# On-demand float32 gather for expert pairs, and nine prefetch places instead of six, in a two-layer trunk with an expert-choice MoE

## What is computed

```python
cap = CAPACITY_FACTOR * T // N_EXPERTS
aff = jax.nn.softmax((h @ w_router).astype(jnp.float32), axis=-1)
g, idx = lax.top_k(jnp.swapaxes(aff, 1, 2), cap)
xg = jax.vmap(lambda xb, ib: xb[ib])(h, idx)
a = jnp.einsum('becd,edf->becf', xg, w_gate)
u = jnp.einsum('becd,edf->becf', xg, w_up)
y = jnp.einsum('becf,efd->becd', jax.nn.silu(a) * u, w_down) * g[..., None].astype(h.dtype)
return jax.vmap(lambda yb, ib: jnp.zeros((T, D), yb.dtype).at[ib.reshape(-1)].add(yb.reshape(-1, D)))(y, idx)
```

## Time and profile before

| what | us |
|---|---|
| median of 3 runs | 1944.04 (1941.34 to 1945.4) |
| the profiled execution | 1943.38 |
| its span | 1941.6 |
| TensorE matmul busy | 1756.0 (90%) |
| VectorE, ScalarE, GpSimd busy | 640.1, 548.5, 514.2 |
| moved by DMA | 567.78 MB |

### The profile page before, as it was taken

How to read it: one execution, slowest core, us unless ns; L and a number is a source line. 1 busy time by engine, 2 the same in 40 slices (tenths; PEclk the granted TensorE clock), 3 DMA queues, 4 the chain that set the end, 5 groups by cost and what they waited for, 6 DMA issues and landing times.

```text
span 1941.6 us, 22758 instructions
## 1 busy us (share of the span) xinstructions
PE 1756.0 (90%) x9190; PEld 1121.8 (58%) x9190; DVE 640.1 (33%) x1385; ACT 548.5 (28%) x1054; POOL 514.2 (26%) x654
## 2 busy tenths in 40 slices
PE   6999999999998888888889999999999978888887
PEld 3888997898542222222268889879965322222223
DVE  3196345873300000001144853558641000000011
ACT  4434353342321110110144344433332111111011
POOL 1787244373100000000047754424830000000000
PEclk9999999999999999999999999999999999999999
DMA  9635434556999999999963354354656999999996
GB/s 359 160 109 196 156 124 151 182 219 235 364 388 427 426 427 428 426 427 426 411 203 130 109 200 164 116 183 171 247 206 261 426 427 426 426 426 427 428 426 251
DMA packets 121512, 567.78 MB, mean 292 GB/s; under 512 B 21824, under 2 KB 31296, under 8 KB 96320
## 3 DMA queue, kind: packets, MB, share of 16 engines
q1 hardware_dynamic: 110624, 543.91, 70.8%
q10 hardware_dynamic: 9920, 20.84, 2.9%
q0 software_dynamic: 864, 1.58, 0.2%
HBM read 550.57 MB, written 15.73 MB: 292 GB/s over the span
## 4 chain that ended last, share of the span: by engine, by line
PE 55%; DMA 35%; DVE 7%; ACT 2%; issue 1%; POOL 0%; ACTq 0%; SPq 0%; DVEq 0%
PE banks L806 29%; PE banks L1376 11%; DMA work<-in_w_gate 8%; DMA ring<-in_w_up 6%; DMA work<-in_w_up 6%; DMA ring<-in_w_down 6%; DMA ring<-in_w_gate 4%; DMA work<-in_w_down 3%; PE banks L1124 1%; PE banks L1345 1%; PE banks L812 1%; PE banks L818 1%; PE banks L838 1%; ACT work L1481 1%; PE banks L1140 1%; DMA work<-in_x_sample 1%
## 5 line engine op out<-in xcount | busy, mean ns | idle before, releaser
L747 POOL TENSOR_TENSOR ring_fp32r<-ring,ring_fp32r 128x256 fp32r<-128x256 f32 x592 | 462.4, 815 | 825.8 <-ACT ring_fp32r L1481 825.1
L1376 PE MATMUL banks<-ring,work 128*64 128x512 f32 x1776 | 404.2, 599 | 77.2 <-DMA ring<-in_w_gate 33.0
L806 PE MATMUL banks<-xT_fp32r,ring_fp32r 128*128 128x384 f32 x1280 | 346.4, 343 | 1.9 <-POOL ring_fp32r L747 1.9
L1481 ACT ACTIVATE work<-banks 32x512 f32<-32x512 f32 (+6 forms) x400 | 202.8, 528 | 438.6 <-PE banks L1376 251.0
L1376 PEld LDWEIGHTS banks<-ring,work 128*64 128x64 f32 x1776 | 122.9, 137 | 336.6 <-issue 200.2
L1376 PE MATMUL banks<-work 128*64 128x512 f32 x972 | 225.5, 600 | 38.6 <-DMA work<-in_w_gate 13.8
L806 PEld LDWEIGHTS banks<-xT_fp32r,ring_fp32r 128*128 128x128 f32 x1280 | 234.9, 190 | 12.8 <-issue 5.3
L806 PE MATMUL banks<-hT_fp32r,ring_fp32r 128*128 128x384 f32 x640 | 215.9, 337 | 0.0
L2406 DVE SCALAR_TENSOR_TENSOR xT<-banks,mod,xT 128x128 f32<-128x128 f32 (+1 forms) x128 | 47.1, 413 | 443.5 <-PE banks L1412 443.1
L1481 ACT ACTIVATE ring_fp32r<-ring 128x1024 fp32r<-128x1024 f32 (+1 forms) x164 | 154.4, 970 | 76.5 <-PE banks L806 66.7
L1376 PEld LDWEIGHTS banks<-work 128*64 128x64 f32 x972 | 67.4, 137 | 178.7 <-issue 112.4
(11 more groups left out here) (298 smaller groups left out, 1702.4 us busy)
## 6 DMA issues: line engine op xcount, KB each, us to landing
ring<-in_w_up SPq DMA_DIRECT2D x38, 2048.0 KB, 30.6
ring<-in_w_gate SPq DMA_DIRECT2D x37, 2048.0 KB, 30.5
ring<-in_w_down SPq DMA_DIRECT2D x36, 2048.0 KB, 30.0
ring<-in_w_in SPq DMA_DIRECT2D x28, 2048.0 KB, 8.4
ring<-in_w_ada SPq DMA_DIRECT2D x20, 2048.0 KB, 8.5
work<-in_w_down SPq DMA_DIRECT2D x20, 2048.0 KB, 30.5
work<-in_w_gate SPq DMA_DIRECT2D x18, 2048.0 KB, 30.5
work<-in_w_up SPq DMA_DIRECT2D x16, 2048.0 KB, 30.6
```

The lines of the kernel that those rows point to most:

```text
L747: ins = pool.tensor_tensor(rounded(w_), w_, rounded(hi_), ALU.subtract)
L806: mm = pe.matmul(dst, a_, b_, start=(first and i == 0), stop=(last and i == 2))
L1376: mm = pe.matmul(dst[64 * hf:64 * hf + 64, :], x(k), w[kk][:, 512 * hf:512 * hf + 512], start=(k == 0), stop=(k == KC - 1), tile_position= ...
L1481: return act.activation(dst, src, ACT.Copy, scale=scale)
```

## The change

The tokens of each pair of experts are gathered in plain float32 when they are needed. H2MH, GpSimd's low parts, the xf detour with its transposes and the one big gather go. `gather(pair, half)` has twelve matmuls of 64 columns (four strides, three token tiles), with the strided H2M stationary; pair 0 is done ahead of expert 0, pair 1 after `expert_u(0)` and in e = 1, and the rest one half after each `expert_u`. XG shrinks to two pairs, SEL to two pairs, SELG to four experts. The gate matrices are turned four experts at a time (`TURN_GATES`), three transposes each. The room holds slots 4, 6, 7 and 8. Slot 8 is used once (half 0), then its place takes YS and YP; the other eight are reused in turn.

```diff
-SLOTS = RING + 3
-FIRST_SLOTS = ((4, 3, 2, 5, 0, 1), (4, 1, 2, 3, 0, 5))
+SLOTS = RING + 5
+FIRST_SLOTS = ((8, 4, 6, 7, 3, 2, 5, 0, 1), (8, 4, 6, 1, 7, 2, 0, 3, 5))
...
+    return FIRST_SLOTS[l][i] if i < 9 else FIRST_SLOTS[l][1 + (i - 9) % 8]
...
+TURN_GATES = (3, 7, 11, 14)
```

The SP queue in layer 0 (`if l < L - 1`), then in layer 1, then for both:

```diff
                     sp.wait_ge(sem["bp_evac"], 8 * (l + 1))
                     load_rows(l, 0)
+                    load_rows(l, 1)
                     sp.wait_ge(sem["wo_out"], 8 * l + 4)
                     load(("mix", l, 28), dr["w_ada"][l + 1], 512)
+                    load_rows(l, 2)
+                    load_rows(l, 3)
                     sp.wait_ge(sem["wo_out"], 8 * (l + 1))
                     load(("mix", l, 29), dr["w_ada"][l + 1], 1024)
-                    load_rows(l, 1)
+                    load_rows(l, 4)
                     sp.wait_ge(sem["ada_part"], EARLY * (l + 1) + 1)
                     load(("mix", l, 30), dr["w_ada"][l + 1], 1536)
                     sp.wait_ge(sem["ada_part"], EARLY * (l + 1) + 2)
-                    load_rows(l, 2)
+                    load_rows(l, 5)
                     sp.wait_ge(sem["h2t_out"], 6 * (l + 1))
-                    load_rows(l, 3)
-                    load_parameters(l + 1)
+                    load_rows(l, 6)
                     sp.wait_ge(sem["ada_part"], EARLY * (l + 1) + 3)
-                    load_rows(l, 4)
+                    load_rows(l, 7)
                     sp.wait_ge(sem["ada_part"], EARLY * (l + 2))
-                    load_rows(l, 5)
+                    load_rows(l, 8)
                 else:
                     sp.wait_ge(sem["bp_evac"], 8 * (l + 1))
-                    load_rows(l, 0)
-                    load_rows(l, 1)
+                    for i in range(5):
+                        load_rows(l, i)
                     sp.wait_ge(sem["wo_out"], 8 * l + 4)
-                    load_rows(l, 2)
+                    load_rows(l, 5)
                     sp.wait_ge(sem["wo_out"], 8 * (l + 1))
-                    load_rows(l, 3)
-                    load_rows(l, 4)
+                    load_rows(l, 6)
+                    load_rows(l, 7)
                     sp.wait_ge(sem["h2t_out"], 6 * (l + 1))
-                    load_rows(l, 5)
-
-                for i in range(6, NW):
-                    if i == 10:
-                        sp.wait_ge(sem["sgt_out"], 3 * (l + 1))
+                    load_rows(l, 8)
+
+                for i in range(9, NW):
                     load_rows(l, i)
+                    if i == 24 and l < L - 1:
+                        load_parameters(l + 1)
```

TensorE:

```diff
+                def gather(pair, half):
+
+                    bank = 2 + half if pair == 0 else 7
+                    pe.wait_ge(sem["sel_ready"], 8 * l + pair + 1)
                     for c in range(4):
+                        for o, ts in ((0, (1, 2)), (64, (0,))):
+                            for t in ts:
+                                mm = pe.matmul(PS[:, bank, 128 * c + o:128 * c + o + 64], strided(H2M[:, t, 512 * half:512 * half + 512], c),
+                                               SEL[pair % 2][:, t, :, :].rearrange("p a b -> p (a b)"), start=(t == ts[0]), stop=(t == ts[-1]))
                     mm.then_inc(sem["xg_out"], 1)
...
+                def gather_next(pair, half):
+
+                    pe.wait_ge(sem["xg_evac"], 16 * l + 2 * pair + half)
+                    if combined[0]:
+                        pe.wait_ge(sem["x_ready"], 32 * l + combined[0])
+                    gather(pair, half)
...
+                gather_more()
                 for e in range(1, NE):
                     units = COMBINED.get(e, ())
                     expert_a(e)
                     if units:
                         combine_early(units[0])
-                    if e == 1:
-                        pe.wait_ge(sem["sgt_evac"], 3 * (l + 1))
                     expert_down(e - 1)
                     if units:
                         combine_early(units[1])
+                    if e == 1:
+                        gather_more()
                     expert_u(e)
+                    gather_more()
+                    if e in TURN_GATES:
+                        turn_gates(TURN_GATES.index(e))
```

More of the change, by code:

```diff
@@ L409, in trunk_program @@
         GT = [v.rearrange("p (a b) -> p a b", a=3) for v in GT]
-        RSTD = W2[:, 0:T]
+        RSTD = work[:, 0:T]
         QF = QKT.rearrange("p a b -> p (a b)")
@@ L424, in MPL @@
             return KRAW if i < 3 else NAQK[:, 1:3, 256:512]
-        m = region(0, WORK)
-        XG = m([KC, NE, 2, 32])
-        base_sel = m.at[0]
+        m = region(0, base_qk + KC * T)
         H2M = m([TT, D])
-        H2MH = m([TT, D])
-        SEL = m([TT, NE, 32])
-        SELG = m([TT, NE, 32])
+        XG = [m([KC, 2, 2, 32]) for _ in range(2)]
+        base_hidden = m.at[0]
+        HH = m([2, 512])
+        HTT = m([2, 4, 128])
+        SEL = [m([TT, 2, 32]) for _ in range(2)]
+        SELG = m([TT, 4, 32])
+        SG = m([2, T])
         POS = m([TT, NE])
         AFF = m([TT, NE])
+        base_topk = m.at[0]
         AFT = m([T])
@@ L438, in trunk_program @@
         MSK = m([T])
-        end_sel = m.at[0]
-        HH = m([2, 512])
-        HTT = m([2, 4, 128])
+        m = region(base_topk, base_topk + 3 * T)
         TH = m([512])
         SA = m([512])
-        end_hidden = m.at[0]
-        SLOT4 = m([SLOT])
+        m = region(base_qk + KC * T, WORK)
         SLOT5 = m([D])
[L448 to L454, removed]
+        EXTRA = {4: m([SLOT]), 6: m([SLOT]), 7: m([SLOT])}
+        base_y = m.at[0]
+        EXTRA[8] = m([SLOT])
+        m = region(base_y, WORK)
+        YS = m([2, D])
+        YP = m([2, D])
         RRAW = AFT
         def MPE(layer):
-            v = work[:, base_gates:base_gates + 2048] if layer == 0 else work[:, end_hidden - 1024:end_hidden]
+            v = work[:, base_gates:base_gates + 2048] if layer == 0 else work[:, base_hidden:base_hidden + 1024]
             return v.rearrange("p (a b) -> p a b", b=512)
@@ L466, in expert_rows @@
                 return [hT[:, 0:8, :].rearrange("p a b -> p (a b)")[:, D * k:D * k + D] for k in range(3)] + [SLOT5]
-            v = ring[:, slot, :] if slot < RING else (SLOT4 if slot == 4 else SLOT6)
+            v = ring[:, slot, :] if slot < RING else EXTRA[slot]
             return [v[:, D * k:D * k + D] for k in range(4)]
@@ L594, in load_rows @@
                     return
-                dst = ring[:, slot, :] if slot < RING else (SLOT4 if slot == 4 else SLOT6)
+                dst = ring[:, slot, :] if slot < RING else EXTRA[slot]
                 sp.dma_start(dst, w.rearrange("(p k) n -> p (k n)", k=4)).then_inc(landed[slot], 16)
@@ L783, in _ @@
                 low_parts(NQ)
[L784 to L789, removed]
             for n, k in (("k", 2), ("v", 2), ("C", 4), ("m", 2), ("ssm", 1)):
@@ L1337, in strided @@
                     return v.rearrange("p (n k) -> p k n", k=4)[:, c, :]
[L1339 to L1348, removed]
@@ L1352, in _ @@
[L1352 to L1359, removed]
@@ L1369, in project @@
+                combined = [0]
+                gather(0, 0)
+                gather(0, 1)
+                def project(dst, i, x, gathered=None):
                     for half in range(2):
+                        if gathered is not None:
+                            pe.wait_ge(sem["xg_evac"], gathered + half)
                         slot, v = LANDING[("expert", l, i + half)]
@@ L1397, in expert_down @@
                         pe.wait_ge(sem["ht_evac"], g)
+                    turned = sum(at < e + 1 for at in TURN_GATES)
+                    if turned:
+                        pe.wait_ge(sem["sgt_evac"], 4 * l + turned)
                     for c in range(4):
@@ L1421, in _, with gather_more @@
                     ada_select(l + 1, 3)
-                pe.wait_ge(sem["xg_evac"], 18 * l + 2)
                 expert_a(0)
                 expert_u(0)
-                pe.wait_ge(sem["sel_ready"], 3 * (l + 1))
                 if l < L - 1:
                     pe.wait_ge(sem["ada_taken"], EARLY * (l + 2))
[L1429 to L1443, removed]
+                gathered = [2]
+                def gather_more():
+                    if gathered[0] < 16:
+                        gather_next(gathered[0] // 2, gathered[0] % 2)
+                        gathered[0] += 1
+                gather_more()
                 for e in range(1, NE):
@@ L1771, in _ @@
                     act.wait_ge(sem["h2t_out"], 6 * l + g + 1)
-                    copy(rounded(H2MH[:, t, 512 * half:512 * half + 512]), PS[:, g, :])
                     copy(H2M[:, t, 512 * half:512 * half + 512], PS[:, g, :]).then_inc(sem["h2t_evac"], 1)
@@ L1776, in _, with take_gathered @@
                     ada_evacuate(l + 1, 3)
-                for half in range(2):
-                    act.wait_ge(sem["xf_out"], 2 * l + half + 1)
-                    copy(XF[0:64, half, :], PS[0:64, half, :]).then_inc(sem["xf_evac"], 1)
```

(52 more changed lines are left out.)

48 lines of the change are left out of this document (16 added, 32 removed).

## The result

The changed kernel takes 2012.99 us (median of 4 runs, 2010.94 to 2017.38) against 1943.8 us of the kernel before: a ratio of 1.0364, 95% interval 1.035 to 1.0378. I had forecast 1919. The profiled execution is the slowest of the four (span 2015.6, before 1941.6), so its stages sum to some 74 us more where the medians say 69.

What follows compares the result with a forecast made beforehand. The DMA stream of weight halves was taken to bound the expert stages. Nine halves ahead give -10.3 us in layer 0 and -14.2 in layer 1, together -24.5 from 1943.4: 1918.9, said as 1919, range 1912 to 1934.

Steps and rivals of the forecast that it cites:

- The bound: Expert stages: the DMA stream of 96 weight halves sets their end; nine halves ahead shorten its last hole.
- rival C: First gathers run at the lower clock or leave small holes: 6 us a layer, 1931 us; chance 0.10.
- The gather's price: Float32 gather on TensorE: 24 records at 0.119 us, 2.9 us a gather; ends 2.7 and 5.5 us.
- g: Time of one gather of twelve float32 matmuls, 24 records on TensorE: put at 2.9 us.
- the 22 us of cover: Layer 1: TensorE's expert work would end at 1885, the weight stream at 1907, hiding 1.6 us more per gather.
- rival A: TensorE becomes the bound: H2M loads at 0.231 us, gathers of 5.5 us, +6.5 us, 1950 us; chance 0.09.
- Its start of the experts: Under slow H2M loads of 0.231 us, the experts start at 521.7 in layer 0 and 1472.1 in layer 1.
- The parameters: Next layer's parameters, moved into the full stream at half 24: 4.2 us put down, ends 1.7 and 10.1.
- Rival B: Parameters cost the whole SP queue hold, stopping the stream up to 10 us: 1925 us; chance 0.17.
- Half 12 and half 16: Weight stream: their places free at S plus 20.4 and 38.5, DMA ready at 21.9 and 41.6; no hole.
- Rival D: Half 9 or those behind it wait for something else in order; no change, 1943 us; chance 0.05.
- the old hole: Weight stream before the change: half 10 goes out behind the gather, at 544.24 and 1493.08, after the stream's last hole.

Runs made afterwards that it cites:

- the contiguous kernel: The changed kernel with H2M written by ScalarE in the order the gather reads it, so the gather's stationary operand is contiguous: 1919.4 us, ratio 0.9872.
- the run with 128 columns: The changed kernel, stride of four kept, with each gather matmul moving 128 columns of SEL instead of 64: 1960.75 us, ratio 1.009.

## Why the prediction was wrong

**The bound, right.** The stream of weights ruled the kernel before, and more places shorten its last hole. With the gather made cheap, the kernel takes 1919.4 us where the sum of the prediction gives 1919. That it is so close is partly luck. Layer 1 of the contiguous kernel needed 445.1 us from the first gather to the last landing where I had 1907.0 - 1460.3 = 446.7, 1.6 us less. Layer 0 needed 967.0 - 510.2 = 456.8 where I had 961.1 - 508.8 = 452.3, 4.5 us more: its first experts took 16.75 us on the chain, against 13.88 in layer 1, at a granted clock of 0.73 from 518 to 528 us (the slow first expert of rival C), and the parameters cost more than I put down. The runs on that chip were 1 us faster to begin with.

**The gather's price, wrong: the step that failed.** "I take 0.119, since it has the type and the stride of the new one." The row was one of transposes, and a transpose does not pay for a stride as a matmul does. The other row, the old gather at 0.231, I called a far end since its 448 columns were part of its pace; yet it was the row with the same operand and the same kind of instruction, and the truth was 0.234: g = 5.79 us for 2.9. With it the 22 us of cover were gone and TensorE became the bound. Of two rows that disagree, the same operand under the same instruction was the nearer one, and the rule of the Trainium skill's page "SBUF — State Buffer" stood on its side.

The trace of the kernel before could have told. 24 records of 384 columns took 4.17 us in the projections (L806), 0.174 us each, so 448 columns by themselves come to 0.174 x 448 / 384 = 0.203 us, less than 0.231; the run with contiguous fp32r operands then took just that, (9.53 - 0.37) / 45 = 0.204. And its load records say where the rest comes from, contiguous in the projections and strided in the gather:

```profile
L806 PEld LDWEIGHTS banks<-work_fp32r,ring_fp32r x768: 186/188/192, 405.9 to 1430.8; 128*128 128x128 f32 x192
...
L1345 PEld LDWEIGHTS banks<-work_fp32r x96: 308/330/337, 530.3 to 1490.3; 128*128 128x128 f32 x96
```

The 0.007 us that I read as the price of the stride compared transposes with matmuls; against contiguous transposes it is 0.011.

**No term for the clock, wrong.** The fall of the clock behind each gather, 24 us in layer 0 and, by the run with 128 columns, 52 us in all, was in no term and in no rival but as the lower clock at the first gathers and 3 us for a slow first expert (C). So rival A, the mechanism that happened, was mis-sized: 1950 where it came to 2013. Without the clock it would have been 1961 (the run with 128 columns), 11 us over rival A, whose g was 5.5 us for 5.79 (and whose terms add up to 457 us, not 456). Its start of the experts, 521.7, was met (522.8).

**The parameters, mis-sized.** 4.2 us put down; the move ahead of the experts saved 9 us by the medians (1919.4 to 1910.3, on two chips whose kernels before differ by 0.5), 6.5 of it in the time from half 9 to the last landing (439.4 to 432.9 us in layer 0). The SP queue was held 16.8 us (594.6 to 611.35), not 10.1. Rival B had this mechanism, at 6 us more than the forecast.

**The rest.** The experts of the contiguous kernel started at 517.7 in layer 0 for 516.4. Half 12 and half 16 opened no hole. Rival D did not happen. What is left of the old hole lies ahead of half 9: from 518 to 528 us in the contiguous kernel the DMA moved nothing, all nine halves being in.

## What to carry to other kernels

Lay the stationary operand of a matmul out so that at least two of its float32 values share 16 bytes; where a copy out of PSUM makes it anyway, the permutation was free here (the ScalarE copies of 128 x 512 took 601 ns before and 595 ns permuted; stride four to one was worth 94 us). When small matmuls go between large ones, count what they do to the clock behind them, not their own time alone. And put loads of many small rows where the queue has nothing else to issue: that was worth 9 us here.

## What the runs showed of the hardware that I had not expected

- Float32 matmuls of 64 columns with a 128 x 128 stationary operand come 0.11 us a record apart at a stride of one, 0.12 at two and 0.23 at four; fp32r ones of 448 columns come 0.23 apart at a stride of four and 0.20 at one. Transposes come 0.12 apart at a stride of four and 0.11 at one.
- The granted clock fell in gathers of 64 columns under loads of 0.23 us, at each of the fourteen of a layer, but neither with 128 columns under the same loads nor with 64 under loads of 0.11. Around the first experts of layer 0 it also fell in kernels without slow float32 gathers, the contiguous one and the one before among them (64 records in 16.75 and 15.36 us); why is not shown.
- One and the same load of small rows held the SP queue for 0.98 to 23.36 us, in full streams never under 9.62; a half of 2048 KB is issued in 0.33 us.
